# Front of a decoder step: the first weight panel's wide transfer moved behind the first input tile, its narrow columns issued from ScalarE's queue

## The reference

```python
def even_layer(x, ...):
    h = rmsnorm(x, norm_g)
    q, kvc, kvs, kvw, gt, z, xbc, dtr = split_cols(h @ w_in, EVEN_SPLITS)
    # attention over compressed, selected and window rows; state-space heads; output projection
```

## Time and profile before

| | |
|---|---|
| time, median of 3 runs | 2839.2 us (2837.57 to 2841.16) |
| the profiled execution, its own time | 2837.64 us |
| its span, first to last instruction | 2836.0 us |
| TensorE busy | 2788.8 us, 98% of the span |
| VectorE, ScalarE, GpSimd busy | 1013.0, 645.7, 731.7 us |
| granted TensorE clock, mean | 0.998 of 2.4 GHz |
| HBM traffic | 162.44 MB read, 19.51 MB written |

### The profile page before, as it was taken

The page is one execution under the profiler, slowest core; times in us unless marked ns, Lnnn a source line. Parts: engine busy times, 40 slices in busy tenths (PEclk is TensorE's granted clock), DMA queues, the critical chain, the costliest instruction groups (busy, mean ns, idle before and its releaser), DMA issues.

```text
span 2836.0 us, 44691 instructions
## 1 busy us (share of the span) xinstructions
PE 2788.8 (98%) x18772; PEld 2534.2 (89%) x18772; DVE 1013.0 (36%) x2138; ACT 645.7 (23%) x1346; POOL 731.7 (26%) x495
## 2 busy tenths in 40 slices
PE   8999999999999999999999999999999999999999
PEld 6866676667689999999999999879999999999998
DVE  3122357776554322222222251383432222222224
ACT  4022214666532100000000031283200000000004
POOL 1430000112322222222222231244222222222221
PEclk9999999999999999999999999999999999999999
DMA  7754212100631111111111112100111111111111
GB/s 236 197 174 145 58 31 63 55 25 2 198 108 45 45 45 45 45 45 45 45 45 45 45 45 53 37 17 16 45 45 45 45 45 45 45 45 45 45 60 64
DMA packets 205898, 179.73 MB, mean 63 GB/s; under 512 B 36730, under 2 KB 186287, under 8 KB 205106
## 3 DMA queue, kind: packets, MB, share of 16 engines
q1 hardware_dynamic: 195184, 144.20, 17.1%
q0 software_dynamic: 7616, 30.14, 3.5%
q10 hardware_dynamic: 2898, 2.54, 0.3%
HBM read 162.44 MB, written 19.51 MB: 64 GB/s over the span
## 4 chain that ended last, share of the span: by engine, by line
PE 71%; DVE 2%; ACT 1%; issue 0%; POOL 0%; DVEq 0%; POOLq 0%; ACTq 0%
PE ps L2322 55%; PE ps L2358 4%; PE ps L2338 4%; PE ps L3026 1%; PE ps L2746 1%; PE ps L2606 1%; PE ps L2727 1%; PE ps L2710 1%; PE ps L1971 1%; PE ps L1959 1%; PE ps L2006 0%; DVE arena L2835 0%; DVE arena L2433 0%; PE ps L3017 0%; PE ps L1988 0%
## 5 line engine op out<-in xcount | busy, mean ns | idle before, releaser
L2322 PE MATMUL ps<-spot,w_hi 128*128 128x352 f32 (+1 forms) x6156 | 1520.5, 327 | 1.4 <-DVE arena L2449 0.7
L2322 PEld LDWEIGHTS ps<-spot,w_hi 128*128 128x128 f32 x6156 | 1082.7, 188 | 2.3 <-DVE arena L2449 1.3
L2322 PE MATMUL ps<-spot,w_lo 128*128 128x368 f32 (+1 forms) x3132 | 1020.2, 326 | 0.0
L2322 PEld LDWEIGHTS ps<-spot,w_lo 128*128 128x128 f32 x3132 | 589.9, 188 | 0.0
L2291 POOL CAST w_hi<-arena 128x2048 fp32r<-128x2048 f32 x78 | 151.6, 1943 | 1330.3 <-DMA arena<-in_w_gate_up 760.2
L2299 POOL TENSOR_TENSOR w_lo<-arena,w_hi 128x2048 fp32r<-128x2048 f32 x77 | 360.4, 4680 | 6.2
L2449 DVE TENSOR_TENSOR arena<-arena,ps 128x368 f32<-128x368 f32 (+1 forms) x312 | 147.2, 528 | 423.7 <-PE ps L2322 352.4
L594 PE MATMUL ps<-arena 128*128 128x368 f32 (+1 forms) x768 | 243.6, 475 | 0.0
L2547 ACT ACTIVATE arena<-arena 128x1088 f32<-128x1088 f32 x44 | 49.0, 1113 | 830.9 <-DVEq L2563 830.9
L594 PEld LDWEIGHTS ps<-arena 128*128 128x128 f32 x768 | 145.1, 192 | 85.5 <-issue 4.8
L2567 DVE TENSOR_TENSOR arena<-arena,ps 128x368 f32<-128x368 f32 x132 | 62.4, 528 | 442.7 <-PE ps L2322 437.6
(11 more groups left out here) (470 smaller groups left out, 3020.2 us busy)
## 6 DMA issues: line engine op xcount, KB each, us to landing
arena<-in_w_gate_up SPq DMA_DIRECT2D x88, 512.0 KB, 4.7
arena<-in_w_down SPq DMA_DIRECT2D x22, 1024.0 KB, 4.9
arena<-in_cache_nsa_slc_kv SPq DMA_DIRECT2D x112, 128.0 KB, 2.5
arena<-in_cache_nsa_cmp_kv SPq DMA_DIRECT2D x109, 128.0 KB, 2.3
arena<-in_w_in_even SPq DMA_DIRECT2D x9, 1024.0 KB, 7.4
x_spill<-arena POOLq DMA_DIRECT2D x1, 4352.0 KB, 13.0
arena<-in_x_prompt SPq DMA_DIRECT2D x8, 512.0 KB, 6.1
arena<-in_cmp_w_k POOLq DMA_DIRECT2D x16, 256.0 KB, 4.4
```

Of the source, the lines that this page charges most:

```text
L2322: mm = nc.tensor.matmul(ps[:, 3 * s + j, 0:b - a], w, x[:, a:b], start=m == 0, stop=m == len(order) - 1)
```

## The change

SyncE issues x tile 0 first, then the identity, then only the wide transfer of panel 0, then x tiles 1 to 7 and the sample tile. ScalarE issues the two narrow transfers of panel 0, between the gains and the page numbers. Nothing is computed otherwise, the number of DMAs and bytes is the same, and all three transfers still raise `w_ready[0]`. TensorE's, VectorE's and GpSimd's instructions and waits are the same ones in the same order.

```diff
         def front_act(act, E):
             load(act, "gains_in")
+            for dst, src in panels[0](w_kv0)[1:3]:
+                act.dma_start(dst, src).then_inc(w_ready[0], 16)
             load(act, "table_in")
             load(act, "setup_in")
...
         def front_sp(sp, weights):
-            load(sp, "ident_in")
             for i in range(NT):
                 src = d["x_prompt"][0, i * P:(i + 1) * P] if i < PT else d["x_sample"].rearrange("b t n -> (b t) n")
                 sp.dma_start(xin[i][0:tile_n(i)], src).then_inc(sem(f"x_in{(i + 1) // 2}"), 16)
-                if i == 2:
+                if i == 0:
+                    load(sp, "ident_in")
                     weights(1)
...
-                    for dst, src in panels[n](wp[n % SLOTS] if n else w_kv0):
+                    for dst, src in panels[n](wp[n % SLOTS]) if n else panels[0](w_kv0)[0:1]:
                         sp.dma_start(dst, src).then_inc(w_ready[n % SLOTS], 16)
```

## The result

| | before | after |
|---|---|---|
| median (lowest to highest), 9 runs each | 2837.57 us (2834.41 to 2846.93) | 2845.85 us (2845.2 to 2856.54) |
| profiled execution, its span | 2836.0 us | 2847.6 us |
| TensorE busy | 2788.8 us | 2788.5 us |
| start of tile 2's transposes | 20.32 us | 30.21 us |

The ratio is 1.0032, with a 95% interval of 1.002 to 1.0044, some 9 us. (Ratios and intervals are the record's, worked out over all runs; they are not the quotient of the two medians, which is 1.0029 here.) It was forecast at 2846.1 us. The head of the page shows that no engine works longer; what grew is TensorE's idle time.

A forecast was written before the change was run, and what follows sets the result against it. TensorE, busy 98% of the span, was taken as the bound. Piece 0 moving from 14.88 to 22.2 gives +7.3, less 0.4 for its slow start: 2839.2 + 6.9 = 2846.1 us, own range 2843.5 to 2849.5, 8-in-10 range 2836.8 to 2849.5.

The forecast's parts named there:

- The sign and the mechanism: Whole kernel: slower, chance 0.50, because narrow packets on ScalarE's queue alternate one for one with SyncE's and delay piece 0.
- Step 1: SyncE's order: wide transfer lands at 9.3 instead of 12.8, x2 at 11.9; piece 0 no earlier than 14.8, against 14.88.
- Step 2: Narrow columns on ScalarE's queue: turns go by packet, so they land at 21.0 us, 6.3 later than before.
- the upper bound of 21.9: Narrow columns' landing if ScalarE's queue gets less than every other packet and they finish only when SyncE's queue is empty.
- Rival A: DMA queues take turns by whole transfers, narrow columns land by about 12: -1.5 us, 2837.7 us; chance 0.20.
- Rival B: DMA turns of some 16 packets, panel at 17.2, piece 0 at 18.4: +3.5, 2842.7 us; chance 0.13.
- Step 3: Behind the narrow columns on ScalarE: x copy delay hidden, setup lands at about 21.2, piece 0 starts at 22.2.
- The -0.4: Piece 0 of the projection: the small matmuls directly ahead may save some of its slow start, -0.4 us.
- The carry to the end: From piece 0 to the end: its shift carries one for one; wrong if the shifts at 25 and 120 us differ.

The follow-up runs named there:

- e2: Kernel before, with only the two narrow transfers moved from SyncE's to ScalarE's queue behind the gains: 2847.67 us, ratio 1.0036.
- e7: e2 with the 32 narrow columns as one transfer of 1024 pieces of 128 bytes, leaving out the time-step columns: 2838.92 us, ratio 1.001.
- e1: Kernel after, but with the narrow transfers on SyncE's queue behind x2, so SyncE's new order alone: 2841.17 us, ratio 1.0003.
- e3: Kernel after, with page numbers and setup rows issued ahead of the narrow transfers on ScalarE's queue: 2849.6 us, ratio 1.0034.
- e4: Kernel after, but with the 8-column narrow transfer on SyncE's queue behind the wide one, the 24-column one staying on ScalarE's: 2843.24 us, ratio 1.0019.
- e8: Kernel before, with the remaining weight panels (from the third) issued ahead of 20 cache pages instead of behind them: 2837.79 us, ratio 0.999.
- e5: Kernel before, with the narrow transfers first on GpSimd's queue with their own semaphore, later x tiles sharing semaphores in threes: 2840.53 us, ratio 1.0003.
- e6: Kernel before, with x tile 1 on its own semaphore and the whole panel 0 issued between x1 and x2: 2841.54 us, ratio 1.0002.
- e9: Kernel before with the edits of e6 and e8 together: 2836.99 us, ratio 0.9985.
- e10: e9 plus the narrow transfers first on GpSimd's queue, x tiles 4 to 8 sharing one semaphore: 2836.28 us, ratio 0.9986.

## Why the prediction was right, and which of its terms were not

**The sign and the mechanism** held. Piece 0 was held back by the narrow columns and by what stands behind them on ScalarE's queue (e2), turns are taken packet by packet (e7, and 211 to 212 after), and the loss reached the end. The time, 2845.85, is within 0.3 us of the forecast, but so close only by luck: the terms gave +6.9, tile 2 shows +9.9, and the medians differ by 8.3. The forecast was laid on the 2839.2 of the three runs shown, and in the nine of the comparison the kernel before had 2837.57; that covered 1.6 us of the miss.

**Step 1** said that the early wide transfer gives nothing: e1 shows that it costs 2.2 us. Sized too small were the landings, the wide transfer at 11.1 (9.3 said) and x2 in time for 14.47 (11.9 said). In e1, without anything on ScalarE's queue beside, tile 1's transposes start at 12.81: 0.9 of the 2.6 is there already, with GpSimd's small loads beside the stream, whose time I had added only at its end; the other 1.7 came with the narrow packets on ScalarE's queue, added at the end as well.

**Step 2**, the narrow columns at 21.0, measured 21.3 for the first and 23.6 for the second. The last one is beyond even the upper bound of 21.9. The stream of x tiles ended near 20 instead of 19.2, which is a small part; the rest is the tail. I left 38 packets per engine, some 600, and let them pass at 1610 a microsecond and land 1.4 later. There were 818 from 20 to 22 us and 129 more behind them, and the landing came at 23.6: the tail was 3.6 us and not 1.8. More were left since the narrow packets began later than at 5.5. By 8 us SyncE's queue had passed 1265 packets, of 1280 for x0, identity and wide transfer. ScalarE's had passed 209, and it has 162 before, without narrow columns; so only some 50 narrow packets (an estimate) had found partners in the wide transfer, where I had counted 30 per engine, 480. The x tiles behind it have 960 packets, and 947 narrow ones were left. And the DMA engines do not finish together: the last 129 packets take 3.6% of 16 engines' time over 2 us, by that share (an estimate) the work of one or two engines.

The equal counts themselves stand in the stretches shown of after, e2, e3 and e7. For 8 to 16 us, the stretch that the prediction named, it is 695 to 649, 7% apart, nearly all of it before 10 us (223 to 183). Rival A (turns of a whole transfer) is refuted by 211 to 212, and the bound named in the prediction, over 1500 packets on ScalarE's queue before 12 us, was far away: there were 556. Rival B, 16 narrow packets against the 8 of one x tile, would show twice as many packets on ScalarE's queue and have brought the panel at 17.2, 6 us earlier than it came.

The Trainium skill, "DMA: Bandwidth & Descriptors", section "Queues, rings and completion order", gives 9 to 17 descriptors for a turn. Between SyncE's and ScalarE's queues the counts of this case don't agree with it: with a mean of 3.6 KB on one side and some 90 bytes on the other they stay equal within one packet from 16 to 18 us. Equal turns of nine on both sides would give that too, but not what steps of 0.1 us show. From 16 to 17 us the two queues count 12 and 13, 8 and 8, 12 and 12, 14 and 13, 7 and 10, 16 and 13, 6 and 6, 11 and 13, 7 and 6, 12 and 12. By its share (8.5% for 212 packets) a narrow packet takes some 13 ns, an estimate, so nine in a row on one DMA engine would fall into about one such step. The counts instead follow SyncE's, never more than 3 apart, which speaks for turns of one.

**Step 3** is the step that failed in its reasoning. It allowed an issue on ScalarE at most 3.4 us, as SyncE's of x3 had the earlier trace rows; it was 10.77. That cost nothing, as e3 shows, but by luck: L684 ended at 23.74 and the last narrow columns landed at 23.6, so the late setup row and the late panel ran side by side to within 0.2 us. Setup was said to land at 21.2, and L682 started at 22.73.

**The -0.4** for a shorter piece 0 had the wrong sign: it took 6.68 instead of 5.59, +1.1. The granted clock in the record is 1.00 in that stretch, but the products run at half rate. The kernel after, L590 alone (columns as for e1 above):

```profile
23.70:28.70 5.00, 5.00 (x11) 3.58 (x12) 1.00 0.12 34
```

Ten start within 5.0 us, 0.50 us each, and one overlaps; a later tile's 16 take 4.05, some 0.25 each. That is the same factor of two as in e1 at a recorded 0.50, so I read it as the lower level, 1.2 GHz, which the record does not report here; this is inferred from the rates alone. By the durations (an estimate from them) the first 6 of 16 are slow in e3 and before, and 12 in e4. Idle time ahead does not make a piece slow, against my assumption: 10.38 us idle, 5.52 long (e3); 2.54 idle, 5.59 long (before); 2.60 idle, 6.20 long (e8); none idle, 6.26 to 7.08 (e2, after, e1, e4). Where piece 0 starts earlier than before, a part goes into the piece (e5, 0.45 of 0.95; e6, 0.42 of 2.10; e9, 0.99 of 1.93). What sets the end of the slow part was not tried and stays open.

**The carry to the end** was said to be one for one, and it is where the check named in the prediction came out against it: 9.9 at tile 2, 12.5 at 121 us. The wait for a later weight panel, 0.4 us in the rows before, was taken as fixed. It isn't: it was none in e2, e3, e7 and in e8 and its successors, then 1.77, 2.80, 3.04, 3.23 and 6.36 (e6, e4, after, e5, e1), in profiled runs of kernels that, e8 to e10 apart, differ only at the front. This spread hides differences of 1 to 2 us at the front (e1, e5, e6), and with it gone (e9) the front's gain is kept in the profile: L696 (L694 before) starts at 119.58, 1.4 us earlier, 1.0 from tile 2 and 0.4 from the wait. At the end it is not told apart from e8's.

## What to carry to other kernels

Before a transfer is moved to a second queue, count its pieces, not its bytes: beside a queue that is full of large packets each small piece on ScalarE's queue waited for one large packet, and 128 KB in 2048 pieces took from 3.4 to 23.6 us here. On GpSimd's queue the same pieces went as 80 packets. What is moved takes with it everything queued behind it on its new queue, both the rows that others wait for and the engine's own next instruction. And bringing one of several inputs forward is worth only what the next latest of them leaves: here tile 1's own input, and the tile that shares its semaphore, were put behind it in the same queue.

## What the runs showed of the hardware that was not expected

- An engine's DMA issue can block it for long: ScalarE stood 10.77 us at a row of 0.5 KB behind 128 small pieces per DMA engine in its own queue, and 3.35 us in e2 with the same pieces (4.93 to 8.28). Why so much less there is open.
- GpSimd's queue moved the same 2048 pieces in 6.8 and 7.4 us, with SyncE's order of e2 beside it (e5). It has 640 packets instead of 560, so 80 for the 2048 pieces; ScalarE's queue has 2242 instead of 162.
- The first 16 products of one shape took between 5.52 and 7.08 us and all later ones 4.05, at half rate for the first 6 to 12, while the record has the granted clock at 1.00. After 6.36 us of idle time (e1) the same half rate is recorded as 0.50.
- A queue's last packets come from few engines: after, 184 of ScalarE's pass from 20.25 to 20.5 us at 45.9% of the engines' time, and 31 from 23 to 23.5 at 3.5%.
